# SSM transfers issued from SyncE between the weights' loads, one more product before layer one's first SSM step, output stored in eight pieces

## The chip, the cores and the metric

One core of a Trainium2 chip runs the whole kernel. The metric is the device time in microseconds (us), the median of several executions. Engines are named PE (TensorE), DVE (VectorE), ACT (ScalarE), POOL (GpSimd) and SP (SyncE). PEld is PE's weight load; ACTq and SPq are the DMA-issuing instructions of ACT and SP.

## What is computed

512 tokens of width 1024 pass two hybrid layers, then one layer of a second kind. Cut to what matters here:

```python
for i in range(2):                                   # first_block
    h = rmsnorm(x, norm_mix[i])
    q, k, v, cb, cc, cx, u, g = split(h @ w_in[i])
    y_attn = sliding_window_attention(rope(q), rope(k), v) @ w_attn_o[i]
    y_conv = (cb * short_conv(cc * cx, conv_w[i])) @ w_conv_o[i]
    ys = gelu(s5_ssm(u, ...))                        # 32 groups, 64 complex states, scan over 512 tokens
    y_ssm = (ys * sigmoid(ys @ w_ssm_glu[i])) @ w_ssm_o[i]
    x = x + (gates[0] * y_attn + gates[1] * y_conv + gates[2] * y_ssm) @ w_mix_o[i]
    x = x + (silu(gt) * up) @ w_ffn_out[i]           # gt, up = rmsnorm(x) @ w_ffn_in[i]
x = rmsnorm(x, norm_final)
# second_block: sparse and blockwise attention, cross attention to a memory, squared-ReLU MLP
x = x + square(relu(h @ w_ff_in)) @ w_ff_out         # the last step; x is the output
```

## The kernel before, in words

x lies transposed in the tile X: 128 partitions, eight tiles (KD = 8) of 512 tokens. Every weight matrix is cut into blocks of 128 output columns. `job_plan` lists the products in order; 417 of them have weights of their own (`tile_of` gives each its number, here "weights n"), with K = 1 to 8 blocks of 128 rows. A product in full float32 accuracy is three PE passes for each block (lines 967 to 969): high part by high part, high by low, low by high; with K = 8 it is 24 matmuls of 512 columns. Results go to three banks of psG in turn.

A weight tile passes four engines. SP loads it into one of three raw slots once the low part of weights n - 3 is made (L884). ACT rounds it to the high part (`round_weights`, L1471), right after it has taken the result of product n - 3. POOL makes the low part by subtraction (L906). PE waits for that low part.

In each of the two layers `mixer_plan(l)` writes out by hand the order of products, of 20 SSM steps (`("ssm", t)`, numbered -1 to 18), and of attention units; all engines walk the same list, each doing its part of an entry. The u tiles come first, then q, k, v with their rotations (`rot`: a PE product with a constant, L1244, of a tile that ACT has just copied from PSUM, L1834; DVE combines), then for four tiles the convolution products cc (taken by ACT), cx and cb (taken by DVE), then gates and outputs (g1, co; co has K = 4). From a given number of products on (`ahead`: 9 in layer one, 3 in layer two) one SSM step stands before each product. Layer one's SSM coefficients are prepared by DVE in `prep` entries before that; the last, `prep 4`, makes W1 of tile 0 and clears TO.

The SSM handles four feature tiles a layer (f = 0 to 7 in all), each in four steps t = 4 ft + phase:
- phase 0: PE multiplies X1 by W1 into psS (L1054, after DVE's W1; signals g_out) and transposes WbE into psT (L1060, signals wbt). ACT issues two DMAs that copy the two halves of W1, swapped, into W2, copies psS to Gm (L1599), issues eight DMAs that lay Gm into the Toeplitz tile TO (L1602), and copies psT to WT and WTI (L1605 to L1608, signals wt_sb). DVE computes rotations.
- phase 1: PE transposes the inputs (L1068), ACT copies them to UG (L1615). DVE, once the eight Toeplitz DMAs have landed, builds the next tile's inputs (`build_inputs`).
- phase 2: PE multiplies WT and WTI by UG (L1075, L1076); DVE scans the states into z1 and z2 (`states`).
- phase 3: PE sums TO, z1 and z2 products in psT (L1086, L1089, L1093), after the TO and W2 landings. DVE builds the next W1 (`build_outputs`).

At the end DVE adds the last eight products to X (`residual`, L1951), signals s_y once, and SP stores all of X with one DMA of 2 MB (L891).

Of the kernel before, what the change touches and what calls it, by code (L numbers as in the profile page):

```python
# [20 lines left out]
P = 128  # L21
# [3 lines left out]
KD = D_MODEL // P  # L25
DEPTH = 2
# [5 lines left out]
FF2_CHUNKS = [(0, 8), (8, 8), (16, 8), (24, 8)]  # L32
# [5 lines left out]
SSM_STATE = 64  # L38
SSM_H = 16
SSM_T = 8  # L40
# [13 lines left out]
RAW_SLOTS = 3  # L54
# [24 lines left out]
FEATURE_TILES = 4  # L79
# [3 lines left out]
def mixer_plan(l):  # L83

    first = [("u", l, i) for i in range(4)]
    if l == 0:  # L90
        first += [("prep", "angles"), ("prep", 1), ("q", l, 0), ("q", l, 1), ("rot", l, 0), ("prep", 2), ("v", l, 0), ("rot", l, 1)]
        first += [("prep", 3), ("vt", l), ("q", l, 2), ("q", l, 3), ("rot", l, 2), ("prep", 4), ("k", l, 0), ("rot", l, 3), ("rot", l, 4)]
    else:
        first += [("q", l, 0), ("q", l, 1), ("v", l, 0), ("rot", l, 0), ("vt", l)]
        first += [("q", l, 2), ("rot", l, 1), ("q", l, 3), ("rot", l, 2), ("k", l, 0), ("rot", l, 3), ("rot", l, 4)]
    for i in range(4):
        first += [("cc", l, i), ("cx", l, i), ("cb", l, i)]
    first += [("g1", l, 0), ("co", l, 0), ("g1", l, 1), ("co", l, 1)]
    plan, t, products = [], SSM_FIRST, 0

    ahead, rests = (9, ()) if l == 0 else (3, (3, 7, 11))
    rested = 0
    for key in first:
        if key[0] == "prep":
            plan.append(key)
            continue
        if key[0] not in ("rot", "vt"):
            if products >= ahead and t <= SSM_LAST:
                if t in rests[rested:]:
                    rested += 1  # L110
                else:
                    plan.append(("ssm", t))
                    t += 1
            products += 1
        plan.append(("job", key))

    def step(unit):
        return [("unit", unit)] if unit <= UNITS_SW + 2 else []

    def scale(unit):  # L120
        return [("scale", unit)] if unit < UNITS_SW else []

    job = lambda kind, i: [("job", (kind, l, i))]
    for i in (2, 3):
        for kind in ("g1", "co"):
            if t <= SSM_LAST:
                plan.append(("ssm", t))
                t += 1
            plan += job(kind, i)
    plan += job("g1", 4) + job("co", 4) + job("glu", 0)  # L130
    plan += step(-1) + job("g1", 5) + scale(0) + job("glu", 1) + job("co", 5) + job("glu", 2)
    plan += step(0) + job("g1", 6) + scale(1) + job("glu", 3) + step(1) + job("co", 6) + scale(2)
    unit, pairs = 2, [("g1", "co", 7)] + [("g2", "so", i) for i in range(KD)]
    for n, (gate, out, i) in enumerate(pairs):
        plan += step(unit) + job(gate, i) + scale(unit + 1)
        unit += 1
        if n % 3 != 1:
            plan += step(unit) + job(out, i) + scale(unit + 1)
            unit += 1
        else:  # L140
            plan += job(out, i)
    plan += step(unit) + job("g0", 0) + step(unit + 1) + job("ao", 0)
    for i in range(1, KD):
        plan += job("g0", i) + job("ao", i)
    assert t == SSM_LAST + 1 and unit + 1 >= UNITS_SW + 2
    return plan
# [302 lines left out]
def block_program(nc, wstream, params, ssmp, cmpw, consts, rope2, xT, memT, outT):  # L449
    jobs = job_plan()  # L450
    weights = [j for j in jobs if j[1]]
    offset, number, taken = {}, {}, {}
    tile_of = {key: n for n, (key, *_) in enumerate(weights)}
    at = 0
# [12 lines left out]
    with ctx:  # L467
        def sem(name):
            return ctx.enter_context(nc.semaphore(name))
# [12 lines left out]
        X, _ = place("x", [P, KD, SEQ], F32)  # L482
# [51 lines left out]
        s_took = {"act": sem("product_taken_act"), "dve": sem("product_taken_dve")}  # L534
# [5 lines left out]
        s_toep, s_w2 = sem("toeplitz_landed"), sem("swapped_w_landed")  # L540
        s_cw = sem("cmp_weights_landed")
        s_out = sem("out_landed")
# [8 lines left out]
        s_gh, s_gl, s_read = sem("raw_h_hi_ready"), sem("raw_h_lo_ready"), sem("raw_h_read")  # L551
        s_rs, s_xms, s_hsq = sem("inverse_root_copied"), sem("query_mean_scaled"), sem("hidden_hi_ready")
        s_sqk1, s_sqm1, s_var = sem("squares_scaled"), sem("squares_scaled_summed"), sem("norm1_variance")
        s_y, s_fin = sem("final_x_ready"), sem("final_norm")
        names = ("dt args coef wb w1 g_out g_sb wbt wt_sb u2 u2_sb ug ug_sb e z1 z yc yc_sb yt ypre ys "
                 "ysplit glu_out toep_clear").split()
        v = {n: sem("ssm_" + n) for n in names}
# [177 lines left out]

        norm_before = {tile_of[first_job[name]] + (2 if name == "norm1" else SPLIT_SLOTS + 1): name for name in h_norm}

        def raw_parts(name):

            return (Mh, Ml) if name == "norm2" else (Hh, Hl)  # L740
# [136 lines left out]
        @block.sync  # L877
        def _(sp_eng):

            for n, (key, K, N, who) in enumerate(weights):  # L880
                if n >= RAW_SLOTS:
                    sp_eng.wait_ge(*low_part_made(n - RAW_SLOTS))
                src = wstream[offset[key]:offset[key] + K * P * P].rearrange("(p f) -> p f", p=P)
                sp_eng.dma_start(raw[:, n % RAW_SLOTS, 0:K * P], src).then_inc(s_raw[n % RAW_SLOTS], 16)  # L884
                if n == 0:
                    for i in range(4):
                        sp_eng.dma_start(X[:, 2 * i:2 * i + 2, :], xT[:, 2 * i:2 * i + 2, :]).then_inc(s_x[i], 16)
                if n == RAW_SLOTS:
                    sp_eng.dma_start(CON[:, MATS_N:], consts[:, MATS_N:]).then_inc(s_in, 16)
            sp_eng.wait_ge(s_y, 1)  # L890
            sp_eng.dma_start(outT, X[:, :, :]).then_inc(s_out, 16)  # L891
            sp_eng.wait_ge(s_out, 16)


        @block.gpsimd
# [552 lines left out]
        def _(act):  # L1448
# [138 lines left out]
            def ssm_step(l, t):  # L1587
                f, phase = l * FEATURE_TILES + t // 4, t % 4
                ft = t // 4
                if t == -1:  # L1590
                    inputs_copy(f + 1)
                elif phase == 0 and ft < FEATURE_TILES:
                    act.wait_ge(v["w1"], f + 1)
                    act.wait_ge(v["g_out"], f + 1)
                    lo, up = slice(0, SSM_STATE), slice(SSM_STATE, P)
                    act.dma_start(W2[lo], W1[up, :, 1:SSM_T + 1, :]).then_inc(s_w2, 16)
                    act.dma_start(W2[up], W1[lo, :, 1:SSM_T + 1, :]).then_inc(s_w2, 16)
                    act.wait_ge(v["wbt"], f + 1)
                    do(act.activation(Gm, psS[0:SSM_H, :, :].rearrange("p a (g x) -> p (a g) x", g=4), ACT.Copy), v["g_sb"])  # L1599
                    act.wait_ge(v["toep_clear"], l + 1)  # L1600
                    for j in range(SSM_T):
                        act.dma_start(TO[j * SSM_H:(j + 1) * SSM_H, :, j * SSM_H:],  # L1602
                                      Gm[:, :, 0:(SSM_T - j) * SSM_H]).then_inc(s_toep, 16)
                    w = psT[:, :, :].rearrange("p a (g x) -> p (a g) x", g=4)
                    do(act.activation(WT, w, ACT.Copy))  # L1605

                    do(act.activation(WTI[:, :, 0:HEAD], w[:, :, HEAD:P], ACT.Copy))
                    do(act.activation(WTI[:, :, HEAD:P], w[:, :, 0:HEAD], ACT.Copy, scale=-1.0), v["wt_sb"])  # L1608
                    if ft < 2:
                        i = 3 * GR + SSM_BC * (ft + 2)  # L1610
                        act.dma_start(sp[ft], ssmp[l][:, i:i + SSM_BC]).then_inc(s_ssmp[ft], 16)
                elif phase == 1:
                    if ft < FEATURE_TILES:
                        act.wait_ge(v["ug"], f + 1)
                        do(act.activation(UG[:, :, :].rearrange("p a b -> p (a b)"), psO[:, :], ACT.Copy), v["ug_sb"])  # L1615
                    if ft:
                        act.wait_ge(v["ypre"], f)
                        do(act.activation(ysf[:, ft - 1], ysf[:, ft - 1], ACT.Gelu_apprx_tanh), v["ys"])
                elif phase == 2 and ft + 1 < FEATURE_TILES:
                    inputs_copy(f + 1)  # L1620
                elif phase == 3 and ft < FEATURE_TILES:
                    act.wait_ge(v["yc"], f + 1)
                    for i, s_i in ((0, None), (1, v["yc_sb"])):
                        do(act.activation(Y2[i].rearrange("c j (g h) -> c g j h", h=SSM_H),
                                          psT[half[i], i, :].rearrange("c (g j h) -> c g j h", j=SSM_T, h=SSM_H),
                                          ACT.Copy), s_i)
# [314 lines left out]
        def _(dve):  # L1941
# [689 lines left out]
            for c, (t0, nt) in enumerate(FF2_CHUNKS):  # L2631
# [4 lines left out]
                    tt(Ml[:, t - t0], rawt[:, n % 2, :], Mh[:, t - t0].bitcast(F32), ALU.subtract, s_hid)  # L2636
                for i in range(KD):
                    residual(("fo2", c, i), i)
            dve.sem_inc(s_y, 1)


def cmp_weights(a):
# [33 lines left out]
```

## Time and profile before

| | us |
|---|---|
| median of 3 runs | 2568.18 |
| lowest, highest run | 2559.44, 2568.51 |
| span of the profiled execution, first to last instruction | 2559.6 |
| PE busy in it | 2445.6 (96%) |
| DVE, ACT, POOL busy | 1262.8, 952.4, 1228.7 |

No separate time of the profiled execution is given beside its span, which lies at the lowest run. A product with K = 8 takes about 5.7 us of PE. Layer one's SSM steps fall in about 79 to 260 us of the span, layer two's in about 880 to 1080. A matmul of 512 columns is listed with 0.39 us but starts 0.227 us after the one before, since they overlap. In a timeline a row gives start, duration, engine, line, operation, output<-inputs, how many were merged, and in brackets the idle time before with its releaser.

### The profile page before, as it was taken

To read this page: it belongs to the slowest core of one execution; us is meant where nothing else is said; L and a number is where in the kernel's file an instruction comes from. 1 tells how busy PE (TensorE), PEld (TensorE's weight loads), DVE (VectorE), ACT (ScalarE), POOL (GpSimd) and SP (SyncE) were. 2 spreads that over 40 slices of the span, in tenths; PEclk is the share of its full clock that TensorE was granted. 3 is DMA by queue.
4 is the path that set the end of the run, shared out by engine and by line. 5 is a ranking of instruction groups with operands and counts; after the bars stand their busy time and mean duration, and the time that the engine had idled before them with its cause. 6 is when DMAs were issued, how large, how long until landed. Compare 5 with 4: busy or idle time off the path is not lost. (4 is left out here: it accounts for less than half of the span.)

```text
span 2559.6 us, 33468 instructions
## 1 busy us (share of the span) xinstructions
PE 2445.6 (96%) x12473; PEld 1953.8 (76%) x12473; DVE 1262.8 (49%) x2342; ACT 952.4 (37%) x1490; POOL 1228.7 (48%) x1594
## 2 busy tenths in 40 slices
PE   7999999999999999999999999998888998999998
PEld 5787777888888778876788878877565667788887
DVE  6983653442335668356343243356688844512211
ACT  5333442432322533344232232254336755523321
POOL 3443435555556635353555555565333332555543
PEclk9999999999999999999999999999988999999999
DMA  4232222333322332222233322223210011223222
GB/s 156 83 88 66 87 63 86 105 110 99 99 99 85 104 85 77 81 83 62 88 107 119 100 87 99 93 97 108 90 55 7 2 34 42 96 94 101 96 98 83
DMA packets 80289, 218.60 MB, mean 85 GB/s; under 512 B 15744, under 2 KB 25344, under 8 KB 79616
## 3 DMA queue, kind: packets, MB, share of 16 engines
q1 hardware_dynamic: 60912, 200.96, 24.3%
q10 hardware_dynamic: 19216, 15.51, 2.2%
q8 instruction: 100, 1.64, 0.3%
q14 instruction: 61, 0.50, 0.1%
HBM read 207.78 MB, written 2.10 MB: 82 GB/s over the span
## 5 line engine op out<-in xcount | busy, mean ns | idle before, releaser
L906 POOL TENSOR_TENSOR w_lo<-w_raw,w_hi 128x256 fp32r<-128x256 f32 (+1 forms) x1482 | 1157.7, 811 | 1202.3 <-ACT w_hi L1471 1202.2
L967 PE MATMUL psG<-h_hi,w_hi 128*128 128x512 f32 x1880 | 752.2, 400 | 12.6 <-POOL h_lo L913 3.5
L968 PE MATMUL psG<-h_lo,w_hi 128*128 128x512 f32 x1880 | 736.7, 392 | 0.0
L969 PE MATMUL psG<-h_hi,w_lo 128*128 128x512 f32 x1880 | 735.9, 391 | 0.0
L1471 ACT ACTIVATE w_hi<-w_raw 128x1024 fp32r<-128x1024 f32 (+4 forms) x417 | 404.0, 969 | 501.4 <-PE psG L969 485.3
L967 PEld LDWEIGHTS psG<-h_hi,w_hi 128*128 128x128 f32 x1880 | 356.0, 189 | 105.3 <-issue 17.7
L969 PEld LDWEIGHTS psG<-h_hi,w_lo 128*128 128x128 f32 x1880 | 355.5, 189 | 75.4
L968 PEld LDWEIGHTS psG<-h_lo,w_hi 128*128 128x128 f32 x1880 | 356.0, 189 | 73.1 <-issue 2.7
L967 PE MATMUL psG<-m_hi,w_hi 128*128 128x512 f32 x800 | 311.9, 390 | 1.1 <-DVE m_lo L1951 1.1
L969 PE MATMUL psG<-m_hi,w_lo 128*128 128x512 f32 x800 | 311.5, 389 | 0.0
L968 PE MATMUL psG<-m_lo,w_hi 128*128 128x512 f32 x800 | 311.4, 389 | 0.0
L1951 DVE TENSOR_TENSOR x<-x,psG 128x512 f32<-128x512 f32 x96 | 66.0, 687 | 357.8 <-PE psG L969 357.7
L967 PEld LDWEIGHTS psG<-m_hi,w_hi 128*128 128x128 f32 x800 | 150.2, 188 | 32.4 <-issue 1.3
L969 PEld LDWEIGHTS psG<-m_hi,w_lo 128*128 128x128 f32 x800 | 150.2, 188 | 31.1
L968 PEld LDWEIGHTS psG<-m_lo,w_hi 128*128 128x128 f32 x800 | 150.3, 188 | 31.0
L967 PE MATMUL psG<-b_hi,w_hi 128*128 128x512 f32 (+1 forms) x306 | 118.3, 386 | 0.0
L968 PE MATMUL psG<-b_lo,w_hi 128*128 128x512 f32 (+1 forms) x306 | 112.7, 368 | 0.0
L969 PE MATMUL psG<-b_hi,w_lo 128*128 128x512 f32 (+1 forms) x306 | 112.6, 368 | 0.0
L1915 ACT ACTIVATE raw_tile<-raw_tile 128x512 f32<-128x512 f32 x44 | 27.8, 633 | 202.9 <-DVE raw_tile L1951 202.9
L1861 ACT ACTIVATE raw_tile<-psG,params 128x512 f32<-128x512 f32 x48 | 33.0, 687 | 159.1 <-PE psG L969 144.6
L1951 DVE TENSOR_TENSOR raw_tile<-psG,squares 128x512 f32<-128x512 f32 x44 | 30.4, 691 | 120.2 <-PE psG L969 116.0
L1954 DVE SCALAR_TENSOR_TENSOR tmp<-raw_tile,psG 128x512 f32<-128x512 f32 x32 | 22.0, 688 | 129.3 <-PE psG L969 129.3
(356 smaller groups left out, 2718.7 us busy)
## 6 DMA issues: line engine op xcount, KB each, us to landing
w_raw<-wstream SPq DMA_DIRECT2D x327, 512.0 KB, 3.3
w_raw<-wstream SPq DMA_DIRECT2D x64, 256.0 KB, 2.6
w_raw<-wstream SPq DMA_DIRECT2D x16, 384.0 KB, 3.0
work_b<-work_b ACTq DMA_DIRECT2D x16, 256.0 KB, 3.7
work_b<-cmpw ACTq DMA_DIRECT2D x2, 2048.0 KB, 8.2
x<-xT SPq DMA_DIRECT2D x4, 512.0 KB, 7.9
small_work<-ssmp ACTq DMA_DIRECT2D x8, 256.0 KB, 2.6
outT<-x SPq DMA_DIRECT2D x1, 2048.0 KB, 6.3
```

The costliest lines, as they stand in the source:

```text
L906: ins = pool.tensor_tensor(lo[:, c], w[:, c], hi[:, c].bitcast(F32), ALU.subtract)
L967: pe.matmul(out, whi, hi, start=(k == 0), stop=False)
L968: pe.matmul(out, whi, lo, start=False, stop=False)
L969: ins = pe.matmul(out, wlo, hi, start=False, stop=(k == K - 1))
L1471: act.activation(hi, raw[:, n % RAW_SLOTS, 0:K * P], ACT.Copy).then_inc(s_hi, 1)
L1861: do(act.activation(rawt[:, n % 2, :], bank, ACT.Tanh, bias=par(("b_gate", l), int(kind[1]) * KD + key[2]), scale=0.5), s_took["act"])
L1915: do(act.activation(rawt[:, n % 2, :], rawt[:, n % 2, :], ACT.Silu), s_silu)
L1951: do(dve.tensor_tensor(out, a, b, op), s)
L1954: do(dve.scalar_tensor_tensor(out, a, s_, b, op0, op1), s)
```

## The change

Three things. `mixer_plan` puts ten instead of nine products before layer one's steps, so that each step -1 to 18 stands one product later. The ten DMAs of each phase 0, with their waits, leave ACT's step and stand in SP's loop, before the load of weights F + 5, where F is the number of the first product with weights behind the step. At the end SP waits for each of the last eight additions and stores that tile of X by itself, 256 KB each.

```diff
--- before.py
+++ after.py
@@ -98,7 +98,7 @@
     first += [("g1", l, 0), ("co", l, 0), ("g1", l, 1), ("co", l, 1)]
     plan, t, products = [], SSM_FIRST, 0
 
-    ahead, rests = (9, ()) if l == 0 else (3, (3, 7, 11))
+    ahead, rests = (10, ()) if l == 0 else (3, (3, 7, 11))
     rested = 0
     for key in first:
         if key[0] == "prep":
@@ -551,7 +551,7 @@
         s_gh, s_gl, s_read = sem("raw_h_hi_ready"), sem("raw_h_lo_ready"), sem("raw_h_read")
         s_rs, s_xms, s_hsq = sem("inverse_root_copied"), sem("query_mean_scaled"), sem("hidden_hi_ready")
         s_sqk1, s_sqm1, s_var = sem("squares_scaled"), sem("squares_scaled_summed"), sem("norm1_variance")
-        s_y, s_fin = sem("final_x_ready"), sem("final_norm")
+        s_fin = sem("final_norm")
         names = ("dt args coef wb w1 g_out g_sb wbt wt_sb u2 u2_sb ug ug_sb e z1 z yc yc_sb yt ypre ys "
                  "ysplit glu_out toep_clear").split()
         v = {n: sem("ssm_" + n) for n in names}
@@ -734,6 +734,14 @@
             last_product[NEXT_NORM[l]] = ("fo", l, len(FFN_CHUNKS) - 1)
 
         norm_before = {tile_of[first_job[name]] + (2 if name == "norm1" else SPLIT_SLOTS + 1): name for name in h_norm}
+
+        ssm_before = {}
+        for l in range(DEPTH):
+            plan = mixer_plan(l)
+            for at, (what, t) in enumerate(plan):
+                if what == "ssm" and t % 4 == 0 and t // 4 < FEATURE_TILES:
+                    following = next(key for w_, key in plan[at:] if w_ == "job" and key in tile_of)
+                    ssm_before[tile_of[following] + RAW_SLOTS + 2] = l * FEATURE_TILES + t // 4
 
         def raw_parts(name):
 
@@ -877,7 +885,26 @@
         @block.sync
         def _(sp_eng):
 
+            def swapped_outputs(f):
+
+                lo, up = slice(0, SSM_STATE), slice(SSM_STATE, P)
+                sp_eng.wait_ge(v["w1"], f + 1)
+                sp_eng.wait_ge(v["g_out"], f + 1)
+                sp_eng.dma_start(W2[lo], W1[up, :, 1:SSM_T + 1, :]).then_inc(s_w2, 16)
+                sp_eng.dma_start(W2[up], W1[lo, :, 1:SSM_T + 1, :]).then_inc(s_w2, 16)
+
+            def toeplitz(f):
+
+                sp_eng.wait_ge(v["g_sb"], f + 1)
+                sp_eng.wait_ge(v["toep_clear"], f // FEATURE_TILES + 1)
+                for j in range(SSM_T):
+                    sp_eng.dma_start(TO[j * SSM_H:(j + 1) * SSM_H, :, j * SSM_H:],
+                                     Gm[:, :, 0:(SSM_T - j) * SSM_H]).then_inc(s_toep, 16)
+
             for n, (key, K, N, who) in enumerate(weights):
+                if n in ssm_before:
+                    swapped_outputs(ssm_before[n])
+                    toeplitz(ssm_before[n])
                 if n >= RAW_SLOTS:
                     sp_eng.wait_ge(*low_part_made(n - RAW_SLOTS))
                 src = wstream[offset[key]:offset[key] + K * P * P].rearrange("(p f) -> p f", p=P)
@@ -887,9 +914,10 @@
                         sp_eng.dma_start(X[:, 2 * i:2 * i + 2, :], xT[:, 2 * i:2 * i + 2, :]).then_inc(s_x[i], 16)
                 if n == RAW_SLOTS:
                     sp_eng.dma_start(CON[:, MATS_N:], consts[:, MATS_N:]).then_inc(s_in, 16)
-            sp_eng.wait_ge(s_y, 1)
-            sp_eng.dma_start(outT, X[:, :, :]).then_inc(s_out, 16)
-            sp_eng.wait_ge(s_out, 16)
+            for i in range(KD):
+                sp_eng.wait_ge(s_took["dve"], taken["fo2", len(FF2_CHUNKS) - 1, i][1])
+                sp_eng.dma_start(outT[:, i], X[:, i]).then_inc(s_out, 16)
+            sp_eng.wait_ge(s_out, 16 * KD)
 
 
         @block.gpsimd
@@ -1590,17 +1618,8 @@
                 if t == -1:
                     inputs_copy(f + 1)
                 elif phase == 0 and ft < FEATURE_TILES:
-                    act.wait_ge(v["w1"], f + 1)
-                    act.wait_ge(v["g_out"], f + 1)
-                    lo, up = slice(0, SSM_STATE), slice(SSM_STATE, P)
-                    act.dma_start(W2[lo], W1[up, :, 1:SSM_T + 1, :]).then_inc(s_w2, 16)
-                    act.dma_start(W2[up], W1[lo, :, 1:SSM_T + 1, :]).then_inc(s_w2, 16)
                     act.wait_ge(v["wbt"], f + 1)
                     do(act.activation(Gm, psS[0:SSM_H, :, :].rearrange("p a (g x) -> p (a g) x", g=4), ACT.Copy), v["g_sb"])
-                    act.wait_ge(v["toep_clear"], l + 1)
-                    for j in range(SSM_T):
-                        act.dma_start(TO[j * SSM_H:(j + 1) * SSM_H, :, j * SSM_H:],
-                                      Gm[:, :, 0:(SSM_T - j) * SSM_H]).then_inc(s_toep, 16)
                     w = psT[:, :, :].rearrange("p a (g x) -> p (a g) x", g=4)
                     do(act.activation(WT, w, ACT.Copy))
 
@@ -2636,7 +2655,6 @@
                     tt(Ml[:, t - t0], rawt[:, n % 2, :], Mh[:, t - t0].bitcast(F32), ALU.subtract, s_hid)
                 for i in range(KD):
                     residual(("fo2", c, i), i)
-            dve.sem_inc(s_y, 1)
 
 
 def cmp_weights(a):
```

## Rows read from the trace of the kernel before

**Rows 1.** The page: busy tenths of PE in 40 slices of the span.
```profile
PE   7999999999999999999999999998888998999998
```

**Rows 2.** Windows behind three waits: busy us of each engine, PEclk, DMA, GB/s.
```profile
89.70:96.00 6.30, 6.30 (x33) 5.21 (x34) 5.69 (x10) 1.01 (x1) 1.21 (x2) 0.73 0.56 164
208.00:220.00 12.00, 12.00 (x55) 10.48 (x56) 4.74 (x6) 1.56 (x2) 3.61 (x6) 0.72 0.21 66
946.60:953.00 6.40, 6.40 (x24) 4.69 (x25) 4.89 (x9) 3.57 (x4) 3.70 (x4) 0.73 0.18 58
```

**Rows 3.** Timeline (start, us, operation, idle before) of PE and DVE, layer one's first steps.
```profile
89.70 2.33 PE L1054 MATMUL psS<-work_b 128*16 128x128 f32 x16 [2.73 <-DVE work_b L1951]
...
100.30 0.50 PE L967 MATMUL psG<-h_hi,w_hi 128*128 128x512 f32 x1
...
106.02 0.43 PE L1075 MATMUL psS<-work_m,work_b 128*128 128x64 f32 x2
...
88.48 1.16 DVE L1951 TENSOR_TENSOR work_b<-work_b 128x576 f32<-128x576 f32 x1
```

**Rows 4.** Window in layer one's SSM steps, columns as in rows 2.
```profile
160.00:200.00 40.00, 40.00 (x289) 33.68 (x288) 36.61 (x49) 12.27 (x17) 17.69 (x18) 1.00 0.30 76
```

**Rows 5.** Timeline of PE and of DVE, tiles 2 and 3 of layer one.
```profile
161.80 1.09 PE L1060 MATMUL psT<-consts,work_b 128*128 128x128 f32 x8
...
185.40 1.04 PE L1089 MATMUL psT<-work_b,work_m 128*64 128x128 f32 x16
...
193.99 1.92 PE L1054 MATMUL psS<-work_b 128*16 128x128 f32 x16
...
172.02 0.29 DVE L1957 TENSOR_SCALAR small_work<-small_work,params 128x128 f32<-128x128 f32 x1 [1.34 <-DMA work_b<-work_b]
...
179.34 0.69 DVE L1951 TENSOR_TENSOR work_m<-psS,work_m 128x512 f32<-128x512 f32 x1
...
183.51 0.74 DVE L1954 SCALAR_TENSOR_TENSOR work_b<-psS,params,work_m 128x504 f32<-128x504 f32 x1
184.68 0.69 DVE L1951 TENSOR_TENSOR small_work<-psG,tmp 128x512 f32<-128x512 f32 x1 [0.43 <-PE psG L969]
...
192.31 0.76 DVE L1951 TENSOR_TENSOR work_b<-work_b,work_m 128x576 f32<-128x576 f32 x1
```

**Rows 6.** Timeline of ACT and of PE, tile 3 of layer one.
```profile
198.44 5.20 ACTq L1602 DMA_DIRECT2D work_b<-work_b  x8
...
202.97 0.50 PE L967 MATMUL psG<-b_hi,w_hi 128*128 128x512 f32 x1
...
207.89 0.43 PE L1075 MATMUL psS<-work_m,work_b 128*128 128x64 f32 x2 [1.88 <-ACT work_m L1615]
```

**Rows 7.** Timeline in layer two's tile 1; line L1602, ns min, median, max, and landing.
```profile
937.91 5.17 ACTq L1602 DMA_DIRECT2D work_b<-work_b  x8
...
945.88 0.60 ACT L1834 ACTIVATE raw_tile<-psG 128x512 f32<-128x512 f32 x1 [0.47 <-ACT work_b L1608]
...
946.58 1.13 PE L1244 MATMUL psG<-raw_tile,consts 128*128 128x512 f32 x2 [3.85 <-ACTq L1836]
...
L1602 ACTq DMA_DIRECT2D work_b<-work_b x64: 587/622/1395, 95.0 to 1029.4; - x64
...
DMA to landing us min/median/max: 1.9/2.7/4.4
```

**Rows 8.** The page's DMA issues (KB each, median us to landing), and line L884.
```profile
w_raw<-wstream SPq DMA_DIRECT2D x327, 512.0 KB, 3.3
w_raw<-wstream SPq DMA_DIRECT2D x64, 256.0 KB, 2.6
...
work_b<-work_b ACTq DMA_DIRECT2D x16, 256.0 KB, 3.7
...
outT<-x SPq DMA_DIRECT2D x1, 2048.0 KB, 6.3
...
L884 SPq DMA_DIRECT2D w_raw<-wstream x417: 327/328/488, 0.7 to 2523.5; - x139
```

## The prediction

> **What bounds the kernel now.** First the page's 40 slices: TensorE (PE) is below 9 tenths only in slice 1, slices 28 to 31, 34 and 40 [rows 1]; of these the change touches slice 40 alone, by the last store. So elsewhere only time in which PE stands still, or runs slowly, while the SSM steps are woven in, can be won. I then read the timeline of PE for the waits in brackets. Three belong to the SSM stretches: 2.73 us for a DVE result at L1054 [rows 3], 1.88 us for an ACT copy at L1075 [rows 6], 3.85 us for an ACT take at L1244 [rows 7]. Next the windows behind each of them: the granted clock is 0.73 over 6.3 us, 0.72 over 12.0 us and 0.73 over 6.4 us [rows 2], so parts of each ran at the lower level (1.2 instead of 2.4 GHz) after PE had stood idle. Last the tail: one store of 2 MB takes 6.3 us from issue to landing behind the last addition [rows 8].
>
> **Edit 1, one more product ahead of layer one's first step (9 to 10).** Now PE has finished the rotations at 86.97, waits 2.73 us and starts step 0 at 89.70, when DVE's last piece of W1 (88.48 + 1.16 = 89.64) is there [rows 3]. With product cc0 put in front (5.7 us, as from 100.30 to 106.02) PE is busy from 87.0 to 92.7, 3 us past the time when W1 is ready. What is late next there: nothing, while that slack lasts. Won: the 2.73 us, and with them the slow stretch, (1 - 0.73) x 6.3 = 1.7 us [rows 2]. **4.4 us.** The product itself costs nothing, as it only changes places with the step; cover for its earlier weights is the lead of the loads, three products, and if that were gone PE would wait at L967.
>
> The shift also moves all 20 steps of that layer against the three-product rhythm of the convolution (cc, cx, cb), and there DVE is nearly full: 36.61 of 40 us [rows 4]. I went through the steps by rows. Step 8 now stands behind cb2 and step 7 behind cx2, a pattern that steps 11 and 12 have today: W1 ends at 192.31 + 0.76 = 193.07 for a PE that wants it at 193.99 [rows 5]. The same last piece took 1.16 us for tile 0 [rows 3]; with three pieces of six that slow the slack of 0.9 turns into a loss of 0.3, so I take 0.2. Step 9's DVE part (build_inputs) starts 9.1 us after PE's transposes (172.02 against 162.89), because it waits for the Toeplitz transfers. Today cc3 with no DVE work follows it; afterwards cx3's convolution (3.6 us, from 184.68 to 193.07 less six W1 pieces of 0.79) comes between it and the state scan. Chain from the end of step 8's transposes: 9.1 + 7.3 (build, to 179.34) + 3.6 + 4.2 (scan to z1, 179.34 to 183.51) = 24.2 us; PE wants z1 after 22.5 us (162.89 to 185.40). Loss 1.7 [rows 5], or none if the DVE pieces run a quarter faster, as 0.76 against 1.16 shows that they can [rows 3, 5]; I take 1.0, near the middle. Step 15 follows step 14 after a 4-tile product instead of an 8-tile one: PE has 3.0 (202.97 to 207.89 less the wait of 1.88) and 0.9 for the TO products, DVE needs the same 4.2 [rows 5, 6]: 0.3 lost. With 0.3 for step 12's W1, **lost 1.8 us**, bounds 0.3 and, if one of these stalls also brings a slow stretch of 1.7 to 3.4 us [rows 2], 6.
>
> **Edit 2, the transfers leave ACT.** Per tile ACT issues two W2 and eight Toeplitz transfers; an issue of the latter takes 622 ns in the median, eight about 5.2 us, in which ACT does nothing else [rows 6, 7]. Behind them stand the WT and WTI copies, a weights' rounding, and the next take. In six of the eight tiles nobody on PE notices. In two PE does. (a) Tile 3 of layer one: ACT's issues last from 198.44 to 203.64, the copy of UG comes behind them and five pieces more, and only the short product co0 (3.0 us from 202.97) stands between PE's transposes and the use of UG; PE has waited 1.88 us when it goes on at 207.89 [rows 6]. Without the issues the copy can follow the transposes at once, 0.6 us from 203.0 on, and is there more than 2 us before PE wants it at 206.0: the 1.9 us go and the slow stretch with them, (1 - 0.72) x 12.0 = 3.4 us [rows 2]. **5.3 us.** (b) Tile 1 of layer two: rot4 needs ACT's take of product k0, and only rot3 (1.0 us) stands between them on PE. The take starts at 945.88, behind 5.17 us of issues (to 943.08) and three copies (2.3 us); PE starts rot4 at 946.58 after 3.85 us [rows 7]. Without the issues ACT is through with the copies at 937.9 + 2.3 = 940.2, before k0 ends (941.7, a rotation before the wait began), and the take of 0.60 us with its hand-over ends some 0.3 us behind rot3: 3.6 us, plus (1 - 0.73) x 6.4 = 1.7 [rows 2]. **5.3 us.** What is late next: the take itself, 0.3 us.
>
> What the same work costs on SP: no row shows it. A weights issue takes 328 ns there [rows 8]; the dearest issue of the Toeplitz line on ACT was 1395 ns, the median 622 [rows 7]. I take the median, since the same instruction makes the same pieces, and keep 0.33 and 1.4 as ends: the slack below covers both. SP now stands still for w1, g_out, g_sb and toep_clear before weights F + 5 (F: the product behind the step). Queued behind that wait is only SP's loads. Today the last Toeplitz transfer has landed 9.1 us after PE's transposes [rows 5], so it is issued some 6.4 us after them (2.7 to land [rows 7]); the load goes out then and lands 3.3 us later [rows 8], at 9.7 us. ACT wants it after three products and the two steps between, 3 x 5.7 + 0.7 + 4.2 = 22 us, in most places, and at tile 3 of layer one, where two of the three are short, after 16 us. So it is covered by 6 us at the worst place and by 12 elsewhere, and even eight issues of 1.4 us (6 us more) only use the 6 up: cost 0. The bytes do not change, and the transfers follow a load that has gone out well before them. DVE's and PE's waits for the landings see the same 5.2 us of issues as today.
>
> Two stalls, above, end only when ACT's issuing has ended, and eight issues take 5.2 us while one of them lands in 2.7 [rows 6, 7]. The Trainium skill, "DMA: Bandwidth & Descriptors", section "Issuing engines are not separate DMA queues", says that starting transfers on several engines saves only the sequencer's time, usually small beside the transfer; the trace does not agree for these, and by that rule edit 2 would bring next to nothing.
>
> **Edit 3, output by tiles.** Seven of eight stores go out while products of 5.7 us still run. Behind the last addition lies one of 256 KB. No row shows a 256 KB store; the nearest are a 256 KB load, 2.6 us, and a W2 copy of that size in small pieces, 3.7 us [rows 8]. Against 6.3 us now: 3.7 or 2.6 won; I take **3.7 us** (the load is the nearer one: whole rows of 2 KB a partition). It is the last thing in the program, so nothing can eat it; SP has issued its last load long before.
>
> **Sum.** 4.4 + 5.3 + 5.3 + 3.7 - 1.8 = 16.9 us. The profiled span of 2559.6 becomes 2542.7. That span lies at the lowest of the three runs (2559.44); the median is 8.6 us above, so the forecast for a median is 2568.2 - 16.9 = 2551.3.
>
> **Rivals.**
> - R1, half the gain is eaten in layer one by DVE. The step order there is new, DVE has 3.4 us free in 40 [rows 4], and two or three stalls of 1 to 2 us with a slow stretch behind each (1.9 + 3.4 at most, twice) take 10.6 us instead of my 1.8: gain 8, median 2560. For it: the 24.2 against 22.5 us above. Against: stalls of that size occur today without a slow stretch, and DVE's idle gaps absorb some.
> - R2, the slow stretches stay, since they follow the thin SSM matmuls rather than the idle time: gain 2.7 + 1.9 + 3.6 + 3.7 - 1.8 = 10, median 2558. Against: step 12 of layer one (193.99), with no wait in front, runs at clock 1.00 [rows 4, 5].
> - R3, ACT's issuing was not the cause: another input of the same copies is as late, and the two stalls stay. Gain 4.4 + 3.7 - 1.8 = 6, median 2562. Against: ACT goes from the issues to the late copies without a gap that any engine but its own explains [rows 6, 7]. The rule of the Trainium skill quoted above comes out here.
> - R4, slower. SP's issuing takes the place of the stall: if an issue of such a strided transfer costs SP far more than ACT, weights F + 5 come late at all eight tiles. Up to (22 - 3.3 - 1.2) / 8 = 2.2 us an issue nothing happens at seven of them; at 3 us each (24 + 4.5 - 22 = 6.5) x 7 + 12.5 = 58 us are lost and the kernel takes 2568 + 58 - 17 = 2609. The break-even is near 2.4 us. Against: the longest issue on ACT was 1.395 us [rows 7].
> - R5, the change does not do what it says: the step before product 11 instead of 10 and SP's place before weights F + 5 follow from the plan, so no chance of its own.
>
> **How the numbers follow.** Forecast as summed 0.68, R1 0.14, R2 0.07, R3 0.06, R4 0.03, something else 0.02. The three runs of before differ by 9 us, so even a right sum can come out 6 us off. The forecast's own range is 2544 to 2559; to hold 8 in 10, with the better end (no DVE loss, the lower kind of run) and R1, R2: 2539 to 2561. A measurement of this kernel tells 0.5% (12.8 us) from no change. Of the forecast's 0.68 some 0.08 fall below 12.8, and R1 to R3 lie below it but for 0.03: faster 0.63, same 0.33 (0.08 + 0.24 and a part of the rest), slower 0.04.
>
> **What would show it.** Right: L1054 in layer one without the 2.7 us wait; no wait of L1075 for ACT L1615; rot4 of layer two about 1 us behind rot3; granted clock 1.0 in the windows behind them; ACT with no issues between Gm and WT; the last landing about 3.4 us behind the last addition's end at the most. Wrong: PE waiting at L1089 or L1093 for DVE z1 (R1), clock below 1 without a wait (R2), ACT late with its queue empty (R3), w_hi waiting for w_raw (R4).

## The result and the profile after

The changed kernel takes 2546.08 us (median of 4 runs, 2542.36 to 2547.28) beside 2566.59 us for the kernel before in the same comparison (4 runs, 2559.44 to 2568.51): a ratio of 0.9919, with a 95% interval from 0.9903 to 0.9936. By the ratio that is 20.8 us less, 16.4 to 24.9; the two medians lie 20.5 apart. The forecast was 16.9 us and a median of 2551.3. The profiled spans went from 2559.6 to 2540.2 us, 19.4 less.

The page of the kernel after, beside [rows 1] and [rows 8]:

```profile
span 2540.2 us, 33476 instructions
...
PE   7999999999999999999999999998898898999999
PEclk9999999999999999999999999999988999999999
...
work_b<-work_b SPq DMA_DIRECT2D x16, 256.0 KB, 3.8
...
outT<-x SPq DMA_DIRECT2D x8, 256.0 KB, 2.0
```

The last slice of PE rose to nine tenths, the W2 transfers (work_b<-work_b, 256 KB) now come from SP's queue and land as fast as they did from ACT's, and a store of one tile lands in 2.0 us in the median.

To see where the 19.4 us came from, the same point of the program is compared in both traces. The mark is ACT's first exponent of the attention units' sink in layer one, which comes behind the SSM stretch. Here are the groups of that line, of before and then of after; what counts is the start of the first one, 260.5 and 252.4 us:

```profile
L1649 ACT ACTIVATE stats<-stats x16: 203/203/206, 260.5 to 374.3; 128x2 f32<-128x2 f32 x16
```

```profile
L1668 ACT ACTIVATE stats<-stats x16: 203/204/205, 252.4 to 366.2; 128x2 f32<-128x2 f32 x16
```

| stretch | before | after | won | forecast |
|---|---|---|---|---|
| start to layer one's mark | 260.5 | 252.4 | 8.1 | 4.4 + 5.3 - 1.8 = 7.9 |
| from there to the same mark of layer two | 837.0 | 830.8 | 6.2 | 5.3 |
| from there to the last addition's start | | | 0.7 | 0 |
| last addition's start to the end of the span | 7.5 | 3.1 | 4.4 | 3.7 |

The same marks in other traces of the same code tell how far such a difference can be trusted. The kernel before with only its stores changed has 262.3 for layer one's mark and 838.4 for the next stretch, 1.8 and 1.4 us more than before; four traces of the kernel after and of two variants of it (two stores instead of eight, a longer wait of SP) lie within 0.2 us (252.4 to 252.6).

The timeline of PE, ACT and SP in the kernel after, for the three waits of [rows 3], [rows 6] and [rows 7]:

```profile
92.45 1.92 PE L1082 MATMUL psS<-work_b 128*16 128x128 f32 x16
...
208.02 0.33 PE L1103 MATMUL psS<-work_m,work_b 128*128 128x64 f32 x2
...
933.15 2.02 PE L1272 MATMUL psG<-raw_tile,consts 128*128 128x512 f32 x4
...
200.19 1.03 ACT L1624 ACTIVATE work_b<-psT 128x1024 f32<-128x1024 f32 x1
201.88 0.60 ACT L1627 ACTIVATE work_b<-psT 128x512 f32<-128x512 f32 x1
203.47 0.58 ACT L1634 ACTIVATE work_m<-psO 128x512 f32<-128x512 f32 x1
...
98.52 5.15 SPq L901 DMA_DIRECT2D work_b<-work_b  x8
```

None of the three PE instructions has a bracket with a wait any more (PE's L1082, L1103 and L1272 are L1054, L1075 and L1244 of before). ACT's copy of UG, L1634, starts at 203.47, 4.5 us ahead of the instruction that reads it; in the kernel before PE waited 1.88 us for it. The eight issues, 5.15 us, are SP's.

The windows behind these three places, beside [rows 2], columns as there:

```profile
84.00:100.00 16.00, 16.00 (x83) 12.28 (x82) 15.03 (x20) 6.85 (x9) 7.32 (x8) 1.00 0.35 103
...
200.00:212.00 12.00, 12.00 (x75) 10.30 (x74) 3.37 (x7) 5.88 (x9) 4.23 (x6) 1.00 0.52 128
...
930.00:945.00 15.00, 15.00 (x85) 11.94 (x84) 13.04 (x21) 7.00 (x9) 5.70 (x6) 1.00 0.44 119
```

PE is busy throughout at a granted clock of 1.00. Inside the SSM steps of layer one PE now waits for DVE's z1 at two places (start, us, operation, wait in brackets):

```profile
119.44 1.09 PE L1117 MATMUL psT<-work_b,work_m 128*64 128x128 f32 x16 [1.37 <-DVE work_m L1970]
...
215.93 1.09 PE L1117 MATMUL psT<-work_b,work_m 128*64 128x128 f32 x16 [0.38 <-DVE work_m L1970]
```

### The profile page after: what moved, and what is told of

Read it like the earlier page. It is cut to its first block and busy times, and to the rows that moved or that the text cites. A ratio compares the mean times of both kernels' runs of the same rounds, so it can differ in the third digit from the quotient of the medians.

```text
span 2540.2 us, 33476 instructions
## 1 busy us (share of the span) xinstructions
PE 2438.6 (96%) x12473; PEld 1950.0 (77%) x12473; DVE 1265.8 (50%) x2342; ACT 952.7 (38%) x1490; POOL 1230.3 (48%) x1594
```

## The experiments

The theory on trial is the sum of the prediction: edit 1 wins PE's wait for W1 and the slow stretch behind it, less what DVE loses to the new order; edit 2 wins because ACT gets its time back; SP's issuing is covered; edit 3 wins the difference in landing. The rivals are R1 (DVE eats more), R2 (slow stretches follow the thin matmuls), R3 (who issues makes no difference) and R4 (SP's issuing delays the loads). First each edit by itself, on the kernel before.

**Edit 1 alone.** The kernel before with this line:

```diff
-    ahead, rests = (9, ()) if l == 0 else (3, (3, 7, 11))
+    ahead, rests = (10, ()) if l == 0 else (3, (3, 7, 11))
```

> The kernel before with the first edit alone: ten products ahead of layer one's first step. Theory (the sum of the prediction): the 2.7 us wait of PE for W1 at L1054 and the slow stretch behind it go, 4.4 us; the new order of the steps against the convolution gives back 1 to 2 us as waits of PE for DVE's z1 at L1089; the waits for ACT in tile 3 of layer one (1 to 2 us) and in tile 1 of layer two (3.8 us) stay, since ACT still issues the transfers. Gain 2.5 to 4.4 us, ratio 0.998 to 0.999. Rival (the slow stretches follow the thin matmuls, not the idle time): the clock stays below 1.00 behind step 0 and the gain is 1 us or less.

Measured: 2566.14 us (12 runs) beside 2565.68 (23 runs), ratio 1.0005 (0.9993 to 1.0016): between 4.1 us slower and 1.8 us faster. The expected gain of 2.5 us or more did not come. PE's wait for W1 is gone; here are PE's remaining waits for ACT in the list of waits (total us, times, longest), of the stretches 70 to 130 and 130 to 290 us:

```profile
PE psS L1075 <- ACT work_m L1615: 1.4, 1, 1.4
```

```profile
PE psS L1075 <- ACT work_m L1615: 2.8, 2, 2.4
```

ACT's timeline in tile 0, and PE's windows there (span of the window, PE's busy us, granted clock, DMA share, GB/s):

```profile
95.81 0.60 ACT L1850 ACTIVATE tmp<-psG 128x512 f32<-128x512 f32 x1 [7.59 <-DVE work_m L1951]
...
97.93 1.02 ACT L1599 ACTIVATE work_b<-psS 16x1024 f32<-16x1024 f32 x1 [0.43 <-issue]
98.98 5.18 ACTq L1602 DMA_DIRECT2D work_b<-work_b  x8
...
107.93 0.58 ACT L1615 ACTIVATE work_m<-psO 128x512 f32<-128x512 f32 x1
```

```profile
105.00:110.00 5.00, 3.56 (x23) 1.00 0.26 65
110.00:115.00 5.00, 5.00 (x27) 0.51 0.02 4
115.00:120.00 5.00, 5.00 (x22) 0.81 0.62 203
```

The earlier PE gets to tile 0's step, the earlier it wants the copy of UG, and that stands behind ACT's 5.18 us of issues. PE stands still for 1.44 us (5.00 - 3.56), and then 5 us pass at 0.51 and 5 at 0.81, which costs another (0.49 + 0.19) x 5 = 3.4 us. That is 4.8 us, more than the 4.4 that the edit was to win. The stall of tile 0 was in no row of the kernel before, since PE's slow stretch behind the W1 wait had covered it. Two more things went against the edit in this trace: the stall of tile 3 is 2.4 us instead of 1.9, with 0.79 and 0.69 in the two windows of 10 us from 210 to 230, which is 5.2 us of slow clock instead of 3.4. So its mark of layer one comes at 263.9, later than in both traces of the old order (260.5, and 262.3 below). The expected waits of PE for z1 are not there.

```profile
L1649 ACT ACTIVATE stats<-stats x16: 203/203/205, 263.9 to 377.7; 128x2 f32<-128x2 f32 x16
```

**Edit 2 alone, edit 3 alone.** The first is the kernel after with nine products ahead and one store at the end; the second is the kernel before with the new last loop:

```diff
-            sp_eng.wait_ge(s_y, 1)
-            sp_eng.dma_start(outT, X[:, :, :]).then_inc(s_out, 16)
-            sp_eng.wait_ge(s_out, 16)
+            for i in range(KD):
+                sp_eng.wait_ge(s_took["dve"], taken["fo2", len(FF2_CHUNKS) - 1, i][1])
+                sp_eng.dma_start(outT[:, i], X[:, i]).then_inc(s_out, 16)
+            sp_eng.wait_ge(s_out, 16 * KD)
```

> The kernel before with the second edit alone: the ten transfers of each tile issued by SP, nine products ahead as before, one store at the end. Theory: the waits of PE for ACT at L1075 (1.9 us) and L1244 (3.8 us) go with the slow stretches behind them, the 2.7 us for W1 stays: gain 10.6 us, ratio 0.996. Rival (ACT's issuing was not the cause; only the sequencer's time is saved and that is hidden): gain 0 to 1 us, both waits still there. Rival (SP's issuing delays weights F + 5): POOL's low part is late and PE waits at L967 for w_lo at the eight tiles; slower than before.

> The kernel before with the third edit alone: eight stores of 256 KB, each behind its own addition. Theory: only the last store is exposed, and it lands 2.0 us after its issue as in the changed kernel, against 6.3 us for the whole: gain 4.3 us, ratio 0.998, nothing else in the trace moves. Rival (the stores of the other tiles disturb the last products' weights): a wait of ACT for w_raw before the last products, gain under 3 us.

Measured: edit 2 alone 2553.07 us, ratio 0.9948 (0.9935 to 0.9961), that is 13.3 us (10.0 to 16.7). Edit 3 alone 2559.6, ratio 0.9978 (0.9968 to 0.9988), 5.6 us (3.1 to 8.2), its last store landing in 2.0 us. With 0 for edit 1 the three make 18.9 us, inside the interval of the 20.8 for all three together.

The trace of edit 3 alone is worth a look, because its code up to the stores is that of the kernel before. Its waits of PE from 80 to 110 us, its mark of layer one, and its windows (columns as in [rows 2]):

```profile
PE psS L1055 <- DVE work_b L1952: 2.8, 1, 2.8
...
PE psS L1076 <- ACT work_m L1616: 1.5, 1, 1.5
```

```profile
L1650 ACT ACTIVATE stats<-stats x16: 203/204/205, 262.3 to 376.2; 128x2 f32<-128x2 f32 x16
```

```profile
80.00:120.00 40.00, 35.75 (x224) 28.71 (x223) 36.19 (x50) 12.22 (x17) 19.51 (x19) 1.00 0.28 81
200.00:240.00 40.00, 38.10 (x228) 31.86 (x227) 15.72 (x23) 12.18 (x17) 12.01 (x16) 0.87 0.21 60
920.00:970.00 50.00, 46.10 (x277) 36.17 (x276) 33.06 (x45) 15.80 (x20) 16.01 (x19) 0.90 0.25 75
```

The wait for W1 is there as in [rows 3], but this time the clock behind it is 1.00, and the stall of tile 0, 1.5 us, comes into sight. So the kernel before had three stalls behind ACT's issues, not two, and this trace has two more of 0.2 us each. The two that were known show again, with 0.87 and 0.90. Edit 2 alone has the W1 wait as well:

```profile
PE psS L1081 <- DVE work_b L1969: 2.8, 1, 2.8
```

```profile
80.00:100.00 20.00, 17.23 (x90) 12.95 (x88) 18.82 (x26) 7.48 (x11) 8.41 (x8) 1.00 0.32 80
...
930.00:950.00 20.00, 20.00 (x113) 16.23 (x112) 17.89 (x25) 10.25 (x13) 9.68 (x10) 1.00 0.41 107
```

Again a wait of 2.8 us and a clock of 1.00 behind it. PE's waits for ACT's copies of UG and for its take before rot4 are gone. (With SP issuing, PE has a new wait of 0.7 us for an ACT copy behind layer one's mark, among the attention units.)

**Is it ACT's time, or something else about the queue?** The kernel after, with five idle repeats of the WT copy for each tile, which take up 5.3 us of ACT where 5.9 us of issues (5.2 for the eight, 0.7 for the two W2 transfers) had stood:

```diff
-                    do(act.activation(WT, w, ACT.Copy))
+                    for _ in range(6):
+                        do(act.activation(WT, w, ACT.Copy))
```

> The changed kernel, with ACT kept busy where its issues stood: the copy of psT to WT is made six times instead of once (5 x 1.05 = 5.3 us more of ACT in each of the eight tiles), while SP issues the transfers as in the changed kernel. The result is the same. Theory (what PE waited for was ACT's time): both stalls come back, about 1.5 us in tile 3 of layer one and 3.6 us in tile 1 of layer two, each with its slow stretch: 6 to 10 us slower than the changed kernel, so some 2552 for 2546. Rival (the gain came from where the transfers are queued, not from ACT's time): the time stays at the changed kernel's, within 1 us.

Measured: 2555.43 us (6 runs), ratio 0.9959 (0.9944 to 0.9974), a median 9.4 us above that of the kernel after, and a span of 2552.4 us, 12.2 above. The list of waits, of 70 to 130, 130 to 290 and of layer two, and the window of layer two:

```profile
PE psS L1103 <- ACT work_m L1635: 1.0, 1, 1.0
```

```profile
PE psS L1103 <- ACT work_m L1635: 1.2, 1, 1.2
```

```profile
PE psG L1272 <- ACTq L1856: 3.5, 1, 3.5
```

```profile
920.00:970.00 50.00, 46.51 (x285) 36.95 (x284) 35.95 (x48) 20.34 (x24) 19.26 (x22) 0.93 0.26 75
```

All three stalls are back, at their places, though the transfers leave from SP. In layer two they cost 837.8 - 830.8 = 7.0 us: 3.5 of wait and (1 - 0.93) x 50 = 3.5 of slow clock. In layer one the waits are shorter than before and brought no slow stretch (1.0 us lost there). The other 4.2 us of the 12.2 lie outside these stretches, and the kernel after, profiled again, has as much there (below). It was ACT's time; R3 falls.

**How long may SP's load be late?** Two kernels, the kernel after with SP waiting longer in front of the load of weights F + 5, for e (in the middle of the tile's steps) or for yc (towards their end):

```diff
                     toeplitz(ssm_before[n])
+                    sp_eng.wait_ge(v["e"], ssm_before[n] + 1)
```

> The changed kernel, with SP kept from its next load longer: before weights F + 5 it also waits for step phase 2's products (signal e). Theory (slack as in the prediction): the load then goes out 5.7 + 0.7 + 5.7 + 3.6 = 15.7 us after PE's transposes instead of 6.4 and lands 3.3 us later at 19.0, ahead of the 22 us at which ACT wants it; at tile 3 of layer one 13.0 + 3.3 = 16.3 us against 16 to 17. Cost 0 to 1 us in all, though no longer any reserve. Rival (SP's wait is already on the path): each of the eight tiles pays part of the 9 us, 20 us or more in all.

> The changed kernel, with SP kept from weights F + 5 until phase 3's products are done (signal yc): 5.7 + 0.7 + 5.7 + 4.2 + 5.7 + 2.8 = 24.8 us after the transposes, landing at 28.1 us against the 22 us at which ACT wants it (at tile 3 of layer one 22 against 16). Theory: about 6 us late at each of the eight tiles, less what ACT's and POOL's lead over PE takes up (POOL's low part is ready one to two us before PE wants it only if the chain runs freely; a product is 5.7 us and the high part is made three products ahead, so up to 7 us of the lateness may be hidden). So between 0 and 50 us slower; if the lead of the parts hides it, the waits of ACT for w_raw grow and PE's do not. Rival (the bound of the prediction, 22 us, is where PE starts to lose): 40 to 50 us slower with waits at the first matmul line for w_lo.

Measured: with e 2544.07 us, ratio 0.9918 (0.9899 to 0.9937), as after, 0.9919. With yc 2565.08 us, 0.9995 (0.9985 to 1.0004), 19 us above after. ACT's waits for loads, with e, and then with yc in layer two (the whole run has 11, of 100.4 us), and PE's waits in the latter:

```profile
ACT w_hi L1500 <- DMA w_raw<-wstream: 5.5, 1, 5.5
```

```profile
ACT w_hi L1500 <- DMA w_raw<-wstream: 57.7, 6, 16.2
...
PE psO L1077 <- ACT squares L1644: 5.6, 3, 2.9
PE psG L996 <- ACT work_m L1863: 5.0, 1, 5.0
```

With e, ACT waited 5.5 us for a load in layer one and nowhere in layer two, and PE nowhere for that. With yc, PE was held up not where it needs the late weights, as I had priced it, but by ACT: the rounding that waits for the load stands in ACT's order ahead of copies and takes that PE wants at once. By the marks 3.4 us of it are lost in layer one (255.8 against 252.4) and 14.2 in layer two (845.0 against 830.8). The slack is real, and it ends in a loss of the size of the whole gain.

**Where is the best place for layer one's steps?** With the queue and the stores as in the kernel after: nine products ahead (edits 2 and 3 without edit 1), eleven and twelve. The last two need steps between the products that follow, as 20 steps no longer fit; this is the edit for eleven, and twelve has a step before each of the gate and output products 4:

```diff
-    ahead, rests = (10, ()) if l == 0 else (3, (3, 7, 11))
+    ahead, rests = (11, ()) if l == 0 else (3, (3, 7, 11))
...
+    if t <= SSM_LAST:
+        plan.append(("ssm", t))
+        t += 1
```

> The changed kernel without the first edit (nine products ahead), the transfers on SP and the eight stores as they are. Theory from the single runs (order alone gives nothing, queue alone 13, stores 4 to 6; layer one ends 2.6 us later without the first edit when SP issues): 2 to 3 us slower than the changed kernel. Rival (the 4.4 us of the prediction): 4.4 us slower. Rival (the first edit is worth nothing in company either): equal within 1 us.

> The changed kernel with eleven instead of ten products ahead of layer one's first step, the last step before the gate product 4. This is the third and last phase of the steps against the three-product rhythm of the convolution. Theory (the remaining loss in layer one is DVE's order, 1.8 us at L1117 in two waits): DVE enters with a product more of lead, the wait for z1 in tile 0 goes, another phase meets another short spot: within 2 us of the changed kernel either way. Rival (steps too late): the first glu product waits for the last tile's split on DVE, 3 us or more lost there.

> Eleven products ahead once more, beside the changed kernel on the same chip. Expected from its first trace (0.9 us of waiting for W1 and 0.2 us for z1 in layer one, against 1.8 us for z1 in the changed kernel): 1 to 3 us faster than the changed kernel. Rival: equal, the difference of 3 us between the first medians was chance.

> The changed kernel with twelve products ahead of layer one's first step, the last two steps before the gate and output products 4. Twelve is three more than nine, so the steps meet the convolution as in the kernel before. Theory (the waits for z1 come from the phase of the steps, not from their being late): no wait of PE for z1 in tile 0, and W1 is long ready, so layer one is 1 to 2 us shorter than in the changed kernel, 2544 in all. Rival (the end of the steps gets too close to the glu products): PE waits for ysplit before the first glu product, 3 us or more, and the time is at or above the changed kernel's.

| products ahead | median us (runs) | ratio (95%) | layer one's mark | PE's waits for DVE in layer one |
|---|---|---|---|---|
| 9 | 2547.7 (5) | 0.9934 (0.9922 to 0.9946) | 254.0 | W1 2.7, z1 0.6 and 0.2 |
| 10 (after) | 2546.08 (4) | 0.9919 (0.9903 to 0.9936) | 252.4 | z1 1.4 and 0.4 |
| 11 | 2542.77 (6) | 0.9914 (0.9899 to 0.9929) | 251.5 | W1 0.9, z1 0.2 |
| 11, again | 2544.99 (5) | 0.9924 (0.9911 to 0.9938) | 251.6 | W1 0.9 |
| 12 | 2546.92 (5) | 0.9930 (0.9918 to 0.9943) | 252.5 | z1 0.6, in two, and 0.7 for a take of DVE's |

The lists of waits, with nine ahead and with eleven:

```profile
PE psS L1082 <- DVE work_b L1970: 2.7, 1, 2.7
...
PE psT L1117 <- DVE work_m L1970: 0.6, 1, 0.6
```

```profile
PE psS L1085 <- DVE work_b L1973: 0.9, 1, 0.9
...
PE psT L1120 <- DVE work_m L1973: 0.2, 1, 0.2
```

So edit 1 in company takes away 2.7 + 0.6 + 0.2 us of waits and puts 1.4 + 0.4 in their place: 1.7 us, and the mark moves by 254.0 - 252.4 = 1.6. (With edit 2 alone, also nine ahead, the mark is at 255.0; 0.8 of that 1.0 us arises in the first 60 us of the span, before any step.) One product more would win another 0.9 by the trace. The intervals of the ratios of the four orders overlap, of nine and ten too: the medians of one comparison differ by 1.8 us (2547.7 and 2545.87 for the kernel after again, below), so what edit 1 is worth in company is a reading of the traces. Eleven was to be 1 to 3 us better than ten and came out 0.9 better beside it, and twelve was to be 1 to 2 us better in layer one and is not (252.5), as the waits moved elsewhere. I would not call either a better kernel.

The windows with nine ahead show once more that the W1 wait can pass without a slow stretch, and a layer one without ACT's issues is at full clock:

```profile
80.00:120.00 40.00, 36.63 (x228) 29.52 (x227) 37.12 (x51) 12.12 (x16) 18.64 (x20) 1.00 0.30 84
200.00:240.00 40.00, 40.00 (x259) 33.37 (x258) 15.18 (x22) 11.92 (x17) 16.92 (x22) 1.00 0.26 78
```

**Two stores of four tiles, and the kernel after again.** The first is the kernel after with stores only behind tiles 3 and 7:

```diff
-            for i in range(KD):
+            for i in (3, 7):
...
-                sp_eng.dma_start(outT[:, i], X[:, i]).then_inc(s_out, 16)
+                sp_eng.dma_start(outT[:, i - 3:i + 1], X[:, i - 3:i + 1]).then_inc(s_out, 16)
```

> The changed kernel with two stores of 1 MB instead of eight of 256 KB; the last one holds tiles 4 to 7. Theory (a fixed part and a part by size, from 2.0 us for 256 KB and 6.3 us for 2 MB: 1.4 us and 2.4 us a MB): the last landing 3.8 us after the issue, 1.8 us later than in the changed kernel. Rival (mostly fixed cost up to some size): 2.0 to 2.6 us.

> The changed kernel once more, for its time beside the others on the same chip and for a second trace of the same code. Expected: 2546 within 3 us; the waits of PE in the SSM steps as in the first trace (1.4 us and 0.4 us for z1) and the granted clock 1.00 from 80 to 280 us. Rival (slow stretches come by chance also without a wait): a window below 0.95 there.

The group of the two stores (issue in ns, start of the first and the last, then landing):

```profile
L919 SPq DMA_DIRECT2D outT<-x x2: 338/343/348, 2516.6 to 2538.3; - x2
DMA to landing us min/median/max: 3.9/3.9/3.9
```

A store of 1 MB lands in 3.9 us, between 2.0 for 256 KB and 6.3 for 2 MB. The kernel was run once, with 2544.73 us; the span was 2542.6 us, 2.4 above after, of which the landing explains 1.9. The kernel after again: 2545.87 us, ratio 0.9925 (0.9912 to 0.9937), span 2544.7, mark of layer one 252.6, the same z1 waits of 1.4 and 0.4, granted clock 1.00 in the windows behind the three places. Its span differs by 4.5 us from that of the other profile, with layer one the same within 0.2: a difference of one profile's span below 5 us says nothing here; that of a stretch without slow clock does.

## Why the prediction came out as it did

The direction, the waits that each edit removes and most of the sizes were right; the median came out 5.2 us lower than forecast (2551.3 - 2546.1). Of that, 2.5 us are terms of the sum (19.4 measured in the spans, 16.9 forecast), 1.6 us the median of before, which was 2566.59 and not 2568.18 in the comparison, and 1.1 us that the medians lie 20.5 apart and the spans 19.4. Some of the closeness is luck. The 8.1 us won up to layer one's mark, for 7.9 forecast, are measured against the very profile from which the sizes were read; against the trace of edit 3 alone, the same code up to there, it is 262.3 - 252.4 = 9.9. And edit 1 came out smaller and edit 2 larger than forecast, which cancels in the sum. Term by term:

- **Edit 1, 4.4 - 1.8 = 2.6 us forecast; 1.6 by the traces beside edit 2, 1.3 lost (4.1 lost to 1.8 won) by the times without edit 2.** The 2.7 us of the wait are right. The step that failed is the slow stretch of 1.7 us counted with it: in three traces (edit 2 alone, edit 3 alone, nine ahead) the same wait has a clock of 1.00 behind it. A slow stretch seen once in one profile is not the wait's price each time. The DVE loss of 1.8 is right in size (1.4 + 0.4) and half wrong in place: step 15's 0.3 became 0.4, but the other was to be 1.0 at step 11 and 0.5 at steps 8 and 12, and it is 1.4 in tile 0, at step 3. PE comes there at 118.07, and DVE's z1 is through at 119.4, after a stretch in which DVE has hardly a gap. The window of the kernel after, columns as in [rows 2], and DVE's last instruction for z1:

```profile
90.00:120.00 30.00, 28.63 (x182) 23.78 (x182) 28.29 (x40) 10.23 (x13) 15.75 (x15) 1.00 0.39 107
```

```profile
118.71 0.68 DVE L1970 TENSOR_TENSOR work_m<-psS,work_m 128x504 f32<-128x504 f32 x1
```

  DVE is busy 28.29 of 30 us: a backlog that starts with the late W1. I had gone through the steps from tile 2 on, where my rows were, and had not put tile 0, the one that begins late, through the same sum.
- **Edit 1 by itself, from which 2.5 to 4.4 us were expected,** wins nothing that the runs can tell, and its trace shows why: the third stall behind ACT's issues lies right behind the wait that goes. That edit 2 has to come first is a reading of the traces; by the times a gain of 1.6 us alone is not ruled out (up to 1.8).
- **Edit 2, 10.6 us forecast, 13.3 (10.0 to 16.7) measured.** Layer two: 6.2 us against 5.3; from the trace of edit 3 alone, 838.4, to that of nine ahead, 829.4, it is 9.0, which is the wait of about 4 us and (1 - 0.90) x 50 = 5.0 of slow clock. Layer one, between the same two traces: 262.3 - 254.0 = 8.3 against 5.3, of which 1.5 and 1.9 are waits and (1 - 0.87) x 40 = 5.2 slow clock (8.6; with nine ahead PE waits 0.8 us for z1 in their place). The failed step is "in six of the eight tiles nobody on PE notices": it was five, as tile 0 stalled too, covered in the trace that I read. The slow stretches were also sized from one execution, and their length changes: over the same windows, 200 to 240 and 920 to 970, the kernel before has granted clocks of 0.91 and 0.97, which is 3.6 and 1.5 us, where the trace of edit 3 alone has 5.2 and 5.0. The forecast of 10.6 lies inside the measured interval.
- **SP's cost, 0 forecast, 0 measured.** Here is the group of SP's issues, beside [rows 7]; I had taken ACT's median of 622 ns for it:

```profile
L901 SPq DMA_DIRECT2D work_b<-work_b x64: 577/601/1467, 98.5 to 1014.8; - x64
...
DMA to landing us min/median/max: 1.8/2.4/3.6
```

  A median of 601 ns and a longest of 1467 are far from the break-even of 2.4 us of R4. That the load had slack to spare is shown by the wait for e: its marks are those of the kernel after or better (252.6, then 829.5 against 830.8), and its ratio is the same.
- **Edit 3, 3.7 us forecast, 4.3 measured** in the landing (6.3 to 2.0; 4.4 from the last addition to the end). Of my two neighbours, the load of 256 KB at 2.6 us was the right one and still too high.
- **The rivals.** R1: one stall of 1.4 us and one of 0.4, none with a slow stretch; not the 10.6 us that it needed, though its sign, PE waiting for z1, did appear. R2: the clock is 1.00 in the three windows behind the places of the waits in both traces of the kernel after, and the thin matmuls are the same; it falls. R3 falls by the edit alone and by the ACT copies; the rule of the Trainium skill ("DMA: Bandwidth & Descriptors", section "Issuing engines are not separate DMA queues") that the issuing time is usually small beside the transfer does not hold for these batches: one issue of 0.62 us is less than a quarter of its landing in 2.7, but the ten of a tile take 5.9 us of ACT, and moving them was worth 13.3 us to the whole. R4 falls, as above, but its mechanism exists: with the longer wait it took back all of the gain.

What stays open: why the same wait of 2.7 to 2.8 us is followed by a slow stretch in one trace and by none in three. The runs show that it is so, not what decides it.

## What to carry to other kernels

An engine that issues DMAs is busy for as long as it issues them: look in its timeline for what stands behind a batch of issues, and move the batch to an engine whose next work has slack, whose size one added wait can measure. When a wait and a slow clock behind it cover a second stall, curing the first alone may bring nothing, so walk the new schedule on from the very first step that moves, not from where the rows happen to be. Only the last piece of the output is exposed at the end, so store it in pieces as soon as each is ready.

## What the runs showed of the hardware

- A strided transfer inside SBUF costs its issuing engine 0.6 us, on SP (601 ns in the median) as on ACT (622 ns), where a plain load of 512 KB costs 328 ns [rows 8].
- Stores to HBM from SP's queue landed after 2.0 us (256 KB, the median of eight; the longest 4.6), 3.9 us (1 MB) and 6.3 us (2 MB). An estimate from the first and the last: about 1.4 us and 2.4 us for each MB, which gives 3.8 for 1 MB.
- Behind one and the same wait of 2.7 to 2.8 us the granted clock was 0.73 in one trace (partly at 1.2 GHz), and 1.00 (2.4 GHz throughout) in three; behind a wait of 1.4 us it was 0.51 for 5 us in another, and 1.00 behind the z1 wait of 1.4 us in the kernel after.
- The kernel with all three stalls is less steady: 23 runs of the kernel before lie between 2557.8 and 2573.5 us, the 9 of the kernel after between 2542.4 and 2547.4. That fewer slow stretches are the reason is a guess; the 6 runs of edit 2 alone, which keeps the W1 wait, lie within 1.5 us.
